# The mixers of a two-stream transformer kernel: another order of the projections, and all convolution taps on VectorE

## What is computed

```python
q, k, v, u = split_cols(modulate(x, sh1, s1) @ w_in[l])     # 512, 128, 128, 1024 columns
q = apply_rope(rms(q) * q_gain, cos, sin); k = apply_rope(rms(k) * k_gain, cos, sin)
o_attn = attend_latent(q, [kc, k], [vc, v])                 # 8 heads of 64, 2 key heads
a, gate = split(u, 2); g = a * sigmoid(gate)
y = conv(g, conv_w, 31 taps per channel) + conv_b
o_conv = silu(layer_norm(y, ln_g, ln_b))
x = x + g1 * concat(rms(o_attn) * beta_attn, rms(o_conv) * beta_conv) @ w_o
x = x + g2 * peer(modulate(x, sh2, s2), peer_wq, peer_keys, peer_u, peer_v)
```

## Time and profile before

| | |
|---|---|
| median of three runs | 3115.87 us |
| profiled execution, its own time | 3116.44 us |
| its span | 3114.6 us |
| TensorE busy | 2424.0 us, 78% |
| VectorE busy | 2134.2 us, 69% |
| ScalarE busy | 537.8 us, 17% |
| GpSimd busy | 1581.2 us, 51% |
| mean transfer rate | 334 GB/s |
| mean granted TensorE clock | 0.915 |

### The profile page before, as it was taken

The page is one execution under the profiler, slowest core; times in us unless marked ns, Lnnn a source line. Parts: engine busy times, 40 slices in busy tenths (PEclk is TensorE's granted clock), DMA queues, the critical chain, the costliest instruction groups (busy, mean ns, idle before and its releaser), DMA issues. The chain is left out here.

```text
span 3114.6 us, 25940 instructions
## 1 busy us (share of the span) xinstructions
PE 2424.0 (78%) x8543; PEld 1341.1 (43%) x8543; DVE 2134.2 (69%) x4292; ACT 537.8 (17%) x1173; POOL 1581.2 (51%) x1633
## 2 busy tenths in 40 slices
PE   5986698499798869978857777788798577777776
PEld 2754255367546546756622222232375422222222
DVE  0559669888768887847698875544366988854444
ACT  1220111000012000013221112222123221111111
POOL 1100335666353665511177777767410577777774
PEclk8987796799996979989979999999999799999999
DMA  6526998999898999951199999999730799999997
GB/s 260 217 95 279 394 414 338 391 395 413 350 406 342 387 389 412 398 191 45 44 390 409 409 410 409 409 409 409 313 133 1 296 409 409 409 409 409 409 409 318
DMA packets 254920, 1038.80 MB, mean 334 GB/s; under 512 B 34923, under 2 KB 36818, under 8 KB 238660
## 3 DMA queue, kind: packets, MB, share of 16 engines
q0 software_dynamic: 221184, 805.40, 65.5%
q1 hardware_dynamic: 31528, 229.28, 18.5%
q10 hardware_dynamic: 2076, 2.47, 0.3%
HBM read 1032.61 MB, written 4.44 MB: 333 GB/s over the span
## 5 line engine op out<-in xcount | busy, mean ns | idle before, releaser
L1849 PE MATMUL PS<-W,SCALE 128*128 128x512 f32 x1984 | 967.7, 617 | 340.5 <-DMA W<-in_peer_v,IDX 260.1
L1956 DVE CUSTOM_DVE_ANT_0 W<-W,PS 128x1024 f32<-128x1024 f32 x512 | 610.2, 1219 | 345.6 <-DMA W<-in_peer_u,IDX 344.9
L1849 PEld LDWEIGHTS PS<-W,SCALE 128*128 128x128 f32 x1984 | 347.2, 192 | 957.5 <-ACT SCALE L1899 539.9
L1994 POOL DMA_INDIRECT W<-in_peer_u,IDX x512 | 484.4, 946 | 427.8 <-DVE IDX L1086 247.7
L1994 POOL DMA_INDIRECT W<-in_peer_v,IDX x512 | 488.5, 954 | 170.2 <-issue 129.3
L1690 POOL DMA_INDIRECT ROWS<-in_peer_u,IDX x206 | 206.9, 1005 | 436.6 <-issue 294.0
L1899 ACT ACTIVATE SCALE<-C,COEF 128x128 f32<-128x128 f32 x496 | 197.4, 401 | 987.9 <-PE PS L1849 959.7
L1528 DVE SCALAR_TENSOR_TENSOR PROD<-ROWS,COEF,PROD 128x1024 f32<-128x1024 f32 x203 | 260.7, 1284 | 69.5 <-DMA ROWS<-in_peer_v,IDX 53.4
L1354 PE MATMUL PS<-XT,W 128*128 128x256 f32 x1408 | 307.4, 379 | 0.0
L1690 POOL DMA_INDIRECT ROWS<-in_peer_v,IDX x204 | 233.1, 1142 | 135.6 <-DVE PROD L1528 86.0
L1354 PEld LDWEIGHTS PS<-XT,W 128*128 128x128 f32 x1408 | 268.0, 190 | 46.1 <-issue 10.7
(11 more groups left out here) (291 smaller groups left out, 2457.4 us busy)
## 6 DMA issues: line engine op xcount, KB each, us to landing
W<-in_w_mod SPq DMA_DIRECT2D x12, 4096.0 KB, 13.5
W<-in_w_up SPq DMA_DIRECT2D x44, 1024.0 KB, 12.0
W<-in_w_in SPq DMA_DIRECT2D x21, 2048.0 KB, 10.6
W<-in_w_down SPq DMA_DIRECT2D x22, 1024.0 KB, 8.0
W<-in_peer_wq SPq DMA_DIRECT2D x6, 2048.0 KB, 8.2
W<-in_w_o SPq DMA_DIRECT2D x6, 2048.0 KB, 7.9
W<-in_w_out SPq DMA_DIRECT2D x4, 2048.0 KB, 11.7
W<-in_peer_u,IDX POOLq DMA_INDIRECT x512, 11.5
```

What stands on the lines that cost most here:

```text
L1849: ins = nc.tensor.matmul(PS[:, 4 + 2 * t + h, :], SCALE[:, i % NSCALE, :], row_slot(at[1, g])[:, h * 512:(h + 1) * 512], start=m == 0, sto ...
L1956: nc.vector.tensor_tensor_reduce(row_slot(n), row_slot(n), h_of(t), 1.0, 0.0, ALU.mult, ALU.add, DOT[:, t, m:m + 1]).then_inc(rows_used, 1)
L1994: nc.gpsimd.indirect_dma_start(row_slot(n), None, tables[("peer_u_2", "peer_v_2")[v]], bass.IndirectOffsetOnAxis(IDX[:, t, m:m + 1], 0),). ...
```

## The change

All of it lies in the three mixers.

1. The weight chunks are reordered: u's two halves are chunks 0 and 1, q, k and v are chunks 2 and 3. TensorE waits for both u chunks, projects u blocks 0, 4, 1 and 5, then q, k and v, then blocks 2, 6, 3 and 7 (`U_ORDER`). ScalarE copies in that order. SP's waits for free slots follow; in the context the `w_mod` load of group 3 is now issued after `proj`, and that of group 2 after the last of u.
2. The fourth block's diagonals on GpSimd and its products on TensorE are gone, with bank 5's special turn. VectorE computes all four blocks in two pairs: pair 0 (blocks 0 and 1) with all its 31 taps ahead of the work on q, k and v; pair 1 in the rounds, three taps a round as before. `CONV_STEP` is 11.
3. Silu is ScalarE's own function, on Y in place, after the last exponential. VectorE's three steps are gone; TensorE's turn of Y waits for ScalarE.
4. For the first tile the queries are in three groups, heads 0 and 1, 2 and 3, 4 to 7 (`HEADS`), each with its own copy and its own scores; the scores of a group stand after the first head of the next. The second tile keeps its halves.

```diff
-        CHUNKS2 = [("w_in_2", 0, 512), ("w_in_2", 512, 256), ("w_in_2", 768, 512), ("w_in_2", 1280, 512),
+        CHUNKS2 = [("w_in_2", 768, 512), ("w_in_2", 1280, 512), ("w_in_2", 0, 512), ("w_in_2", 512, 256),
...
-        CONV_STEP = 12
+        HEADS = [[(0, 2), (2, 4), (4, 8)], [(0, 4), (4, 8)]]
+        def heads_up_to(t, h):
+            return sum(len(HEADS[i]) for i in range(t)) + sum(h0 < h for h0, _ in HEADS[t])
+        U_ORDER = [0, 4, 1, 5, 2, 6, 3, 7]
+        CONV_STEP = 11
...
+            def conv_in(at):
+                j = U_ORDER[at]
+                b = banks.take(conv_in_ready, at + 1)
+                matmul_rows(pe, b, (0, S), lambda k: wslot(j // 4, DK, 512)[:, k, (j % 4) * P:(j % 4 + 1) * P],
+                            lambda k: XT[:, k, :], DK).then_inc(groups_done, groups.mark("u", j))
+                groups.at["u", j, "bank"] = b
+            for c in range(2):
+                weights_in(pe, c, first)
+            for i in range(4):
+                conv_in(i)
             for c, (o, n) in enumerate(((0, 512), (512, 256))):
-                weights_in(pe, c, first)
+                weights_in(pe, 2 + c, first)
...
-                                lambda k: wslot(c, DK, n)[:, k, :], DK).then_inc(
+                                lambda k: wslot(2 + c, DK, n)[:, k, :], DK).then_inc(
...
-            for j in range(8):
-                c = 2 + j // 4
-                if j % 4 == 0:
-                    weights_in(pe, c, first)
-                b = banks.take(conv_in_ready, j + 1)
-                matmul_rows(pe, b, (0, S), lambda k: wslot(c, DK, 512)[:, k, (j % 4) * P:(j % 4 + 1) * P],
-                            lambda k: XT[:, k, :], DK).then_inc(groups_done, groups.mark("u", j))
-                groups.at["u", j, "bank"] = b
+            for i in range(4, 8):
+                conv_in(i)
...
-                for k in range(3 * i, min(3 * i + 3, TAPS2)):
-                    pe.wait_ge(diag_ready, k + 1)
-                    if k == 0:
-                        pe.wait_ge(pad_ready, 1)
-                    ins = nc.tensor.matmul(PS[:, 5, 0:S], diag(k), B["PAD"][:, 3, k:k + S], start=k == 0, stop=k == TAPS2 - 1)
-                    if k == TAPS2 - 1:
-                        ins.then_inc(groups_done, groups.mark("conv"))
...
-                    pe.wait_ge(conv_ready, 2)
-                    banks.put_back(5)
+                    pe.wait_ge(conv_ready, 1)
...
-            def scores(t, half):
-                pe.wait_ge(picksT_ready, t * 2 + half + 1)
-                if t == 0 and half == 0:
+            def scores(t, u):
+                h0, h1 = HEADS[t][u]
+                pe.wait_ge(picksT_ready, heads_up_to(t, h1))
+                if t == 0 and u == 0:
                     pe.wait_ge(keysT_ready, 2)
-                bs = [banks.take(score_read, t * 4 + half * 2 + c + 1) for c in range(2)]
-                for i in range(4):
+                done = 2 * (heads_up_to(t, h1) - 1)
+                bs = [banks.take(score_read, done + c + 1) for c in range(2)]
+                for h in range(h0, h1):
+                    o = (h - h0) * P
                     for c in range(2):
-                        h = half * 4 + i
-                        ins = nc.tensor.matmul(PS[:, bs[c], i * P:(i + 1) * P], B["QPT"][c * HD:(c + 1) * HD, t, h, :],
+                        ins = nc.tensor.matmul(PS[:, bs[c], o:o + P], B["QPT"][c * HD:(c + 1) * HD, t, h, :],
                                                B["KPT"][c * HD:(c + 1) * HD, h, :], start=True, stop=True)
-                        if i == 3:
-                            ins.then_inc(groups_done, groups.mark("ps", t, half * 2 + c))
-                            groups.at["ps", t, half * 2 + c, "bank"] = bs[c]
+                        if h == h1 - 1:
+                            ins.then_inc(groups_done, groups.mark("ps", t, u, c))
+                            groups.at["ps", t, u, c, "bank"] = bs[c]
...
-                for j in range(2):
-                    if t == 0:
-                        weights_in(pe, 6 + j, first)
-                    b = banks.take(picksT_ready, t * 2 + j + 1)
-                    groups.at["pq", t, j, "bank"] = b
-                    for h in range(4):
-                        ins = matmul_rows(pe, b, (h * P, (h + 1) * P), lambda k: wslot(2 + j, DK, 512)[:, k, h * P:(h + 1) * P],
+                for u, (h0, h1) in enumerate(HEADS[t]):
+                    if t == 0 and h0 % 4 == 0:
+                        weights_in(pe, 6 + h0 // 4, first)
+                    b = banks.take(picksT_ready, heads_up_to(t, h1))
+                    groups.at["pq", t, u, "bank"] = b
+                    for h in range(h0, h1):
+                        j, i = divmod(h, 4)
+                        ins = matmul_rows(pe, b, ((h - h0) * P, (h - h0 + 1) * P), lambda k: wslot(2 + j, DK, 512)[:, k, i * P:(i + 1) * P],
                                           lambda k: XT[:, k, t * P:(t + 1) * P], DK)
-                        if j == 1 and h == 0:
-                            scores(t, 0)
-                    ins.then_inc(groups_done, groups.mark("pq", t, j))
-                scores(t, 1)
+                        if u and h == h0:
+                            scores(t, u - 1)
+                    ins.then_inc(groups_done, groups.mark("pq", t, u))
+                scores(t, len(HEADS[t]) - 1)
...
-                    last = {4: ("proj", 0, 1), 5: ("proj", 1, 1), 6: ("u", 3), 7: ("u", 7)}[c]
+                    last = {4: ("u", 3), 5: ("u", 7), 6: ("proj", 0, 1), 7: ("proj", 1, 1)}[c]
...
-            for c, (o, n) in enumerate(((0, 512), (512, 256))):
-                for t in range(TT):
-                    b = bank("proj", c, t)
-                    nc.scalar.copy(B["PROJ"][:, t, o:o + n], PS[:, b, 0:n]).then_inc(proj_ready, 1)
-            for j in range(8):
-                if j == 2:
+            for i, j in enumerate(U_ORDER):
+                if i == 4:
+                    for c, (o, n) in enumerate(((0, 512), (512, 256))):
+                        for t in range(TT):
+                            b = bank("proj", c, t)
+                            nc.scalar.copy(B["PROJ"][:, t, o:o + n], PS[:, b, 0:n]).then_inc(proj_ready, 1)
+                if i == 6:
...
-                if i == CONV_STEP - 1:
-                    act.wait_ge(groups_done, groups.of("conv"))
-                    nc.scalar.activation(B["U"][:, 3, :], PS[:, 5, 0:S], ACT.Identity, bias=B["COLC"][:, 3, TAPS2:TAPS2 + 1]).then_inc(conv_ready, 1)
...
-                if i == CONV_STEP + 3:
+                if i == n:
                     act.wait_ge(act_in_ready, 1)
-                    nc.scalar.activation(B["EY"], B["Y"], ACT.Exp, scale=-1.0).then_inc(act_out_ready, 1)
+                    nc.scalar.activation(B["Y"], B["Y"], ACT.Silu).then_inc(act_out_ready, 1)
...
+            def gate_conv(pair):
+                dve.wait_ge(conv_in_ready, 4 * pair + 4)
+                nc.vector.tensor_tensor(B["PAD"][:, 2 * pair:2 * pair + 2, HALO:HALO + S], B["U"][:, 2 * pair:2 * pair + 2, :],
+                                        B["U"][:, 2 * pair + 4:2 * pair + 6, :], ALU.mult).then_inc(pad_ready, 1)
+                dve.wait_ge(pad_ready, pair + 1)
+            def tap_step(pair, k):
+                for j in (2 * pair, 2 * pair + 1):
+                    tap = B["COLC"][:, j, k:k + 1]
+                    if k == 0:
+                        ins = nc.vector.tensor_scalar(B["U"][:, j, :], B["PAD"][:, j, 0:S], tap, B["COLC"][:, j, TAPS2:TAPS2 + 1], ALU.mult, ALU.add)
+                    else:
+                        ins = nc.vector.scalar_tensor_tensor(B["U"][:, j, :], B["PAD"][:, j, k:k + S], tap, B["U"][:, j, :], ALU.mult, ALU.add)
+                if pair == 1 and k == TAPS2 - 1:
+                    ins.then_inc(conv_ready, 1)
+                else:
+                    link(ins)
+            gate_conv(0)
+            for k in range(TAPS2):
+                tap_step(0, k)
...
-            dve.wait_ge(conv_in_ready, 8)
-            nc.vector.tensor_tensor(B["PAD"][:, :, HALO:HALO + S], B["U"][:, 0:4, :], B["U"][:, 4:8, :], ALU.mult).then_inc(pad_ready, 1)
-            dve.wait_ge(pad_ready, 1)
+            gate_conv(1)
...
-            def tap_step(k):
-                for j in range(3):
-                    tap = B["COLC"][:, j, k:k + 1]
-                    if k == 0:
-                        ins = nc.vector.tensor_scalar(B["U"][:, j, :], B["PAD"][:, j, 0:S], tap, B["COLC"][:, j, TAPS2:TAPS2 + 1], ALU.mult, ALU.add)
-                    else:
-                        ins = nc.vector.scalar_tensor_tensor(B["U"][:, j, :], B["PAD"][:, j, k:k + S], tap, B["U"][:, j, :], ALU.mult, ALU.add)
-                if k < TAPS2 - 1:
-                    link(ins)
-                else:
-                    ins.then_inc(conv_ready, 1)
...
-                    tap_step(k)
+                    tap_step(1, k)
...
-            link(nc.vector.tensor_scalar(B["EY"], B["EY"], 1.0, None, ALU.add))
```

(7 more changed lines are left out.)

50 lines of the change are left out of this document (13 added, 37 removed).

## The result

| | before | after |
|---|---|---|
| median of the runs beside each other (5 and 5) | 3116.98 us | 3129.88 us |
| profiled execution, its own time | 3116.44 us | 3127.70 us |
| its span | 3114.6 us | 3125.9 us |
| mean granted TensorE clock | 0.915 | 0.900 |

The changed kernel is **slower**: ratio 1.0039, 95% interval 1.0023 to 1.0056, 12 to 13 us. The forecast was 3107, and the time lies outside its range of 3097 to 3121.

What follows compares the result with a forecast made beforehand. The prediction took VectorE to bound the rounds and TensorE the stretch before them. From 3116.44 us, mixers gave -6.9 + 1.1 + 4.5 = -1.3 and heads -8.0, -9.3 in all: 3107.1, written as 3107, range 3097 to 3121.

Steps and rivals of the forecast that it cites:

- The rounds: Latent mixers' first eleven attention rounds: VectorE paces them at 3.37 us each, 35.2 us in all instead of 47.5.
- Rival (b): Rounds without diagonals: TensorE's clock halves, 5.2 us a round, up to 3147; chance 0.08 slower, 0.07 no change.
- The transposes as the reason: Attention rounds: transposes (0.66 us a round) may not count as clock activity, making the half-clock rival likelier; its chance left unchanged.
- Front of the latent mixers: Projections to maximum 0: first-pair taps take 28.5 us ahead of q, k, v; first maximum 0 at 1425.0, before 1414.2.
- the wait for w_in: Second latent mixer's start: TensorE waits for two weight pieces, 4.7 us later, then a cold start of 1.6.
- Turn of q and k behind 9 us of idle: Latent mixers ahead of maximum 0: after idling, half clock on turn and first score adds 1.7 us, bounds 0 and 3.4.
- Context: Context mixer: later weights, a w_mod wait and longer front, less Silu and norm gains, end it 4.5 us later, bounds 2 and 9.
- the w_mod wait: Context, ahead of the turn of q and k: w_mod, issued after the last of u, lands at 126.3; product 6.4 + 0.6.
- Tail and Silu: Mixer ends: latent tail 14.0 us instead of 15.7; last maximum to turn of Y 5.4 instead of 9.1, 3.7 less.
- A drain of 1.38 us: ScalarE's table load before Silu: possible extra drain per switch, 4.1 us in all, sum 3111; given 0.02, counted within another rival.
- Heads: First tile's key search in latent mixers: starts 4.4 us earlier, 4.0 each come through, 8.0 us in all.
- Rival (a): Search and gathers: TensorE-tied issue of rows 12 and on sets the end, the 8.0 us are lost, 3115; chance 0.18.

Runs made afterwards that it cites:

- e4: The changed kernel plus, in latent mixers, 16 unread matmuls ahead of the turn of q and k and two per round: 3314.01 us, ratio 0.9978, on a slower chip.
- e5: The kernel before with only the Silu part of the change, in all three mixers: 3105.39 us, ratio 0.9956.
- e6: The kernel before with only the heads part, first tile searched in groups of two, two and four: 3113.50 us, ratio 0.9979.
- e7: The kernel before with both the Silu and the heads parts, convolution untouched: 3099.79 us, ratio 0.9942.
- e12: e7 with diagonals kept and 25 taps of one u block moved into VectorE's idle time ahead of the turn: 3064.28 us, ratio 0.9840 to the kernel before.
- e1: The changed kernel plus 16 unread matmuls in TensorE's idle ahead of the turn of q and k, latent mixers only: 3338.25 us, ratio 1.0052, slower chip.
- e2: The changed kernel plus one unread matmul in each latent round, none in the idle ahead of the turn: 3358.28 us, ratio 1.0118, slower chip.
- e8: The changed kernel with Silu and heads taken back, leaving moved taps and projection order: 3156.74 us, ratio 1.0118 to the kernel before.
- e9: The changed kernel with context w_in slots exchanged, so the first-needed w_mod half is fetched earlier: 3116.27 us, ratio 1.0001 to the kernel before.

## Why the prediction was wrong

- **The rounds: the step that failed.** The prediction put "10 x 3.37 + 0.61 + 0.92 = 35.2" for eleven rounds. It is right for VectorE (e4's second mixer: 35.5), but TensorE sets the round, with 4.65 us at half clock: 45.1, or 9.9 too few in each latent mixer. 2 x 9.9 = 19.8; the forecast with them is 3107 + 19.8 = 3127, and measured were 3129.9. The 2.9 that are left are less than what two long stretches that the change doesn't touch brought over their forecast (2.7 and 2.0), and what sets these is open.
- **Rival (b) was this mechanism, with a chance of 0.15 in all.** Its price of 5.2 us a round was a little high, and the first four rounds escape it (3.35, TensorE has no P V yet in three of them). What misled was the argument against it: that a TensorE which is behind no longer idles, and so gets its clock back. Its rows were from the kernel before, where the half clock in the tail ended after 10 us. In the changed kernel TensorE left no gap for 29 us at 0.50. Nothing in the trace before showed a round without a diagonal that had held, or regained, the clock for longer than the last few; the diagonals were counted at nothing "except for the clock", and that exception was the result.
- **The trace before had the hint.** The prediction laid the half clock in its tail to an idle of 1.40 us. But the clock fell ahead of that idle, at 1459.60, behind the last diagonals; in the second latent mixer it fell 8.0 us behind the last one. First TensorE, then the window (columns as above):

```profile
1454.94 0.70 PE L591 MATMUL PS<-ROWS,XT 128*128 128x256 f32 x2
...
1457.39 1.10 PE L620 MATMUL PS<-V,ROWS 128*128 128x64 f32 x8 [1.31 <-ACT ROWS L815]
```

```profile
1459.00:1470.00 11.00, 9.60 (x36) 7.08 (x34) 5.96 (x14) 4.14 (x10) 0.00 (x0) 0.53 0.00 1
```

  In all eight latent mixers of the kernel before, e5, e6 and e7 it fell 3.8 to 8.5 us behind the last diagonal. That was a hint and no proof: these last rounds also idle longer (1.31 us for 0.45 ahead of the P V), and in e12 the clock held for 18.9 us behind the last diagonal.
- **The transposes as the reason: not shown.** The Trainium skill's sentence on them (TensorE: Matmul & The Clock Gate, Part 4: PE-mode transpose) spoke for rival (b), and the rival came true; but no run here changes the transposes alone. The traces rather speak against it: of the 23 latent mixers, over all runs, that came to the turn of the convolution at half clock, 21 were back at full clock 0.1 to 2.4 us behind the eight transposes of this turn (the other two are the first ones of e1 and e2).
- **Front of the latent mixers: right.** Taps 28.3 for 28.5, maximum 0 at 63.5 for 64.2; the wait for w_in in the second mixer 4.4 for 4.7, with a cold start of 2.1 for 1.6 (16.05 us for 64 matmuls, where the last 64 take 13.98). The cold start forecast for the first mixer did not come: its half of u took 14.1 us. That was luck: in e8 and e9 it came, and maximum 0 stood at 65.0 and 65.7.
- **Turn of q and k behind 9 us of idle: right.** From the turn to maximum 0 are 5.7 us, in e1 with a warm TensorE 3.5; the prediction took 1.7 for these 2.1.
- **Context: close by luck.** +5.6 for +4.5, but of terms that miss and cancel. Maximum 0 came at 135.5 for 137.4, since the product behind the wait took 4.97 us for the 6.4 + 0.6 forecast. The rounds to maximum 11 took 37.7 for 34.3: the forecast had 2 us for one w_mod product in them, and both lengthened their round, mostly at half clock (5.7 us each, where the kernel before has 3.66 and 5.34). From the last maximum to the turn of Y are 4.7 us, before 9.3, so the Silu gave back 4.6 for 3.7. e9 shows that the w_mod wait alone is worth 12; the prediction named it and its instant (126.3, measured 126.0).
- **Tail and Silu: right.** 13.0 us and 0.7 for the last maximum make the 13.7 that were forecast as 14.0; 5.1 for 5.4. Alone (e5) the three Silus and the warm turn behind them bring 13 us. A drain of 1.38 us behind each table load, which the Trainium skill gives (ScalarE: Activation LUTs, What ACT_TABLE_LOAD costs), doesn't show: 0.02 us lie between load and Silu.
- **Heads: right.** The search starts 5.7 and 7.0 earlier against Y. Of these, 1.3 and 2.5 lie ahead of the turn of O and come of the full clock (in the second mixer the y products take 14.00 us for 15.43); 4.4 and 4.5 are left for the heads. It comes through to the next layer's issues, 700.8 us behind the search for 700.6 before, though e6 has 702.8 there. Rival (a) falls by e6, whose interval ends at 0.9990.

## What to carry to other kernels

Work that looks free on an engine with time to spare may be what holds that engine's clock: before taking dense matmuls out of a TensorE that runs light, cost the stretch at half clock as well, and don't count on a gapless queue to bring the clock back. Fill the idle time that an engine has ahead of a wait with just as much moved work as fits (25 taps of one block in 13 us), instead of reordering what feeds the others: that keeps weights, transfers and the clock as they are. And when slots are exchanged for a new order, the transfer issued behind the last reader moves too; one such wait was worth 12 us here.
